# Splitting one 2 MB weight transfer at six of 32 experts into 8 + 8 + 112 partitions, in a hybrid decoder step on one Trainium2 core

## The chip, the core and the metric

The program runs on one core of one Trainium2 chip. Time is the device time of the program in microseconds (us). Before the change, three runs gave 1109.86, 1110.63 and 1121.22 us, with a median of 1110.63 us. Engines are named as in the profile: PE is TensorE, DVE VectorE, ACT ScalarE, POOL GpSimd, SP SyncE. SP issues nearly all transfers, and 16 DMA engines carry them.

## What is computed

One decoder layer for 256 prompt tokens and 8 x 4 sample tokens, all in float32: a normalisation and a combined projection, sliding-window attention beside a state-space part, an output projection, and then a mixture of experts. The last part takes most of the time:

```python
h = xb @ w_gate_up[e] + b_gate_up[e]          # 1024 -> 2048
return _clamped_swiglu(h) @ w_down[e] + b_down[e]   # 1024 -> 1024
...
y = jax.ops.segment_sum(out.astype(jnp.float32) * row_w[:, None], row_tok, num_segments=t_)
```

There are 32 experts, each token goes to four of them, and every expert's weights are read once: 8 MB for gate and up, 4 MB for down, 384 MB in all. The state-space part also returns its last states, `h_last`, an array of 128 partitions x 288 numbers (144 KB).

## The kernel before

The core works through the 32 experts one after the other, in 32 "positions". The position says how many tokens the expert is expected to have: `few` (a slim tile of 32 slots), `mid` (a wide tile of 64) or `many` (both). The kinds follow a fixed pattern: two `mid`, then four rounds of `few, many, few, mid`, then two rounds of `few, mid, mid, few, mid, mid`, then two `few`. Every engine runs the rounds as loops (`ROUNDS` = 4 and `LATER` = 2).

Weights go through two rings in SBUF. `gu_ring` has four slots of 2 MB; the four together hold one expert's gate and up weights. `dn_ring` has four slots of 2 MB: slots 0 and 1 take the down weights of even positions, slots 2 and 3 those of odd ones. A slot is 128 partitions x 16 KB, and one transfer fills it: partition p receives 16 KB that lie together in HBM (`load_gu` L341, `load_dn` L346). Before each transfer SP waits until PE has used the slot's old contents: it waits for `gu_used` in `gu` and for `dn_used` in `dn`. For each position SP issues the two down slots and then the four gate-up slots, in a loop at L394 that handles two positions each time and runs 14 times. Positions 0 and 1 are loaded ahead of the loop by `first_gu` (L352) and `first_dn` (L370), the last two behind it.

On PE a position is: `gate_up` (eight pieces of the inner dimension, k = 0 to 7, two for each gate-up slot, waiting for `gu_in` at each slot), turns and gathers, and `down` (four pieces, two for each down slot, waiting for `dn_in` at each slot). In `down` at a `few` position, `slim_part(c)` does piece c; c = 0 waits for the first down slot and c = 2 for the second.

Each transfer raises its semaphore by 16 when it has landed, and one semaphore belongs to one slot.

`h_last` is stored by POOL at its program's end (L2182), as soon as DVE has written it. SP passes a wait for the same event (`hlast_ready`) a little before L352's sixth transfer. Further on, SP waits for `out_done` to reach 64 (four earlier stores have landed) before it overwrites the memory those stores read.

Of the kernel before, what the change touches and what calls it, by code (L numbers as in the profile page):

```python
# [38 lines left out]
MT = 96  # L39
# [2 lines left out]
ITEMS = T * TOPK // SLOTS  # L42
PAIRS = NE // 2
GU_SLOTS = 4
GU_ROWS = KT // GU_SLOTS
FEW = 32
BODY, ROUNDS = ("few", "many", "few", "mid"), 4
# [30 lines left out]
def build(nc, a):  # L78
# [49 lines left out]
    o = REST  # L128
# [140 lines left out]
    for n in ("par_in cols_in b_in ones_in const_in c_in mask_in cache_in wglu_in wout_in "  # L269
              "w1_in late_in out_done "  # L270

              "xsq_ready xg_ready sum_ready ms_ready r_mix_ready u_proj un_ready u_ready proj_done proj_free "
              "sq_ready qk_sum vs_ready rq_ready qk_ready v_ready v_turned v_tok_ready "

              "par_dve par_act w1c_ready v_zero_ready v_power bt_turned bt_ready k_ready kd_ready tz_ready "
              "mag4_ready r_scan_ready x_ready x_free hin_ready hlast_ready "
              "y_done y_ready ysq_ready y_poly tanh_ready gelu_ready "

              "score_ready score_used neg_ready exp_done sum_inv p_ready pt_turned pt_ready pv_ready a_part_ready "
              "asq_ready asum_ready qs_ready av_ready ar_ready cleared outA_done xmid_ready "  # L280

              "glu_done ga_ready th_glu s_ready ssq_ready ssum_ready sv_ready sr_ready sn_ready outB_done x2_ready "

              "x2sq_ready rt_ready x2sum_ready x2v_ready r2sum_ready xn_ready logits_ready xtok_turned xtok_ready top_ready "
              "exp4_done sel_ready pos_ready "

              "bias_turned bias_ready order_ready "
              "first_half first_copied "
              "oh_ready gathered gath_ready xe_turned xe_ready gu_used g_acc g_copied l_copied h_turned "
              "h_step hg_ready th_ready h_ready dn_used ye_ready "  # L290
              "oh_s_ready gather_s copied_s raw_s_ready h_turned_s hg_s_ready th_s_ready h_s_ready ye_s_ready "
              "goh_s_ready g_turned_s gT_s_ready "
              "goh_ready g_turned gT_ready comb_done acc_done "
              "list_ready pos_item_ready h_out "
              "dve_order act_order").split():
        S(n)
    wu_in, wq_in = [S(f"wu_in{c}") for c in range(CT)], [S(f"wq_in{c}") for c in range(3)]
    S("tail_done"), S("dn_last")
# [73 lines left out]
    def load_others(sp):  # L372

        regs = [sp.alloc_register(f"sp_at{k}") for k in range(2)]

        def expert_at(k, p):
            sp.reg_load(regs[k], ord_e[0:1, p:p + 1] if isinstance(p, int) else ord_e[0:1, bass.ds(p, 1)])
            return sp.snap(regs[k], min_val=0, max_val=NE - 1)

        def gu(x, p_before):  # L380
            for k in range(GU_SLOTS):
                sp.wait_ge(S("gu_used"), p_before * 8 + GU_ROWS * (k + 1))
                load_gu(sp, x, k)

        def dn(x, p_before, j):
            for h in range(2):
                sp.wait_ge(S("dn_used"), p_before * 4 + 2 * (h + 1))
                load_dn(sp, x, h, j)

        for r in range(KT):  # L390
            sp.wait_ge(S("gu_used"), r + 1)
            first_gu(sp, 1, [r])
        sp.wait_ge(S("order_ready"), 1)
        with sp.Fori(0, PAIRS - 2) as i:  # L394
            x = [expert_at(k, i * 2 + (k + 2)) for k in range(2)]
            dn(x[0], i * 2, 0)
            gu(x[0], i * 2 + 1)
            dn(x[1], i * 2 + 1, 1)
            gu(x[1], i * 2 + 2)
        x = [expert_at(k, NE - 2 + k) for k in range(2)]  # L400
        dn(x[0], NE - 4, 0)
        gu(x[0], NE - 3)
        gu(x[1], NE - 2)
        for h in range(2):
            sp.wait_ge(S("dn_used"), (NE - 3) * 4 + 2 * (h + 1))
            if h == 0:
                load_dn(sp, x[1], 0, 1)
# [50 lines left out]
    def _(sp):  # L458
# [42 lines left out]
        first_gu(sp, 0, range(0, 5))  # L501
        sp.wait_ge(S("y_done"), 4)
        sp.wait_ge(S("hlast_ready"), 2)
        first_gu(sp, 0, range(5, 6))
        first_dn(sp, 0)
        sp.wait_ge(S("outA_done"), KT)
        sp.dma_start(w_out[:], a["w_out"][:, CT:2 * CT]).then_inc(S("wout_in"), 16)

        sp.wait_ge(S("glu_done"), 8)
        sp.wait_ge(S("out_done"), 64)  # L510
        first_gu(sp, 0, range(6, 8))
        first_dn(sp, 1)
        sp.wait_ge(S("sn_ready"), CT)
# [19 lines left out]
        for k, c in enumerate((0, 2, 1, 3)):  # L533
# [4 lines left out]
        sp.wait_ge(S("out_done"), 16 * 8)  # L538


    @block.tensor
    def _(pe):
# [447 lines left out]
        def down(w, s, kind, after, s_after, j, fill):  # L990

            def wide_part(c):
                if c == 0:
                    pe.wait_ge(S("h_ready"), w + 1)
                if c % 2 == 0:
                    pe.wait_ge(dn_in[2 * j + c // 2], fill * 16)
                for kk in range(2):
                    f = 2 * c + kk
                    for h in range(2):
# [5 lines left out]
            def slim_part(c):  # L1005
# [5 lines left out]
                    pe.wait_ge(S("dn_last"), 16)  # L1011
                if kind == "few" and c % 2 == 0:
                    pe.wait_ge(dn_in[2 * j + c // 2], fill * 16)
                for kk in range(2):
                    f = 2 * c + kk
                    for q in range(4):
# [75 lines left out]
        def expert(p, w, s, kind, before, after, j, fill):  # L1092
# [40 lines left out]
            down(w, s, kind, after, s_after, j, fill)  # L1133

        first_gather()
        turn_first()
# [2 lines left out]
        with pe.Fori(0, ROUNDS) as i:  # L1139
            for k in range(4):  # L1140
                expert(i * 4 + (2 + k), i * (WIDE[6] - WIDE[2]) + WIDE[2 + k], i * (SLIM[6] - SLIM[2]) + SLIM[2 + k],
                       BODY[k], BODY[k - 1], BODY[(k + 1) % 4], k % 2, i * 2 + (k // 2 + 2))
        with pe.Fori(0, LATER) as i:
            for k in range(6):
                p = FIRST_LATE + k
                expert(i * 6 + p, i * (WIDE[p + 6] - WIDE[p]) + WIDE[p], i * (SLIM[p + 6] - SLIM[p]) + SLIM[p],
                       KINDS[p], KINDS[p - 1], KINDS[p + 1], k % 2, i * 3 + (p // 2 + 1))
# [25 lines left out]
    def _(act):  # L1173
# [215 lines left out]
        for u in range(6):  # L1389
# [7 lines left out]
            if u == 3:  # L1397

                act.wait_ge(S("top_ready"), 1)
                A(ex4[0:MT], ex4[0:MT], ACT.Exp).then_inc(S("exp4_done"), 1)  # L1400

        def act_gathered(g):

# [130 lines left out]
    def _(dve):  # L1534
# [391 lines left out]
        dve.wait_ge(S("exp4_done"), 1)  # L1926
# [238 lines left out]
    def _(pool):  # L2165
# [140 lines left out]
```

## Time and profile before

| | |
|---|---|
| median of 3 runs | 1110.63 us |
| the profiled execution's own time | 1110.5 us |
| its span (first to last instruction) | 1108.7 us |
| granted TensorE clock, mean | 0.980 |
| PE busy | 986.8 us (89%) |
| DVE busy / ACT busy / POOL busy | 392.4 / 205.2 / 13.3 us |
| moved by DMA | 425.22 MB |

The page's slice row of DMA shows, for each fortieth of the span (27.7 us), how much of the time the 16 DMA engines were busy on average. A 9 is 90% or more. From the eighth slice on it reads 9 to the last but one. The share of a window is that of all 16 engines together: a 5 in it can mean that each engine works half the time, or that eight of them work and eight have nothing left.

### The profile page before, as it was taken

How to read it: one execution, taken by the hardware profiler on the slowest of the kernel's cores; microseconds unless marked ns; L12 is line 12 of the kernel's file. 1: busy time of each engine (PE TensorE's matmuls, PEld its weight loads, DVE VectorE, ACT ScalarE, POOL GpSimd, SP SyncE). 2: the span in 40 equal slices, each digit the busy share in tenths (PEclk: the TensorE clock that was granted, in tenths of full speed). 3: DMA queues.
4: the chain of work that ended last, by engine and by line, in shares of the span. 5: the costliest groups of instructions: out<-in, count | busy, mean ns of one | idle time of the engine just before them, and what ended most of it. 6: DMA issues, size and time to landing. Idle time of an engine off the chain costs nothing.

```text
span 1108.7 us, 16624 instructions
## 1 busy us (share of the span) xinstructions
PE 986.8 (89%) x6604; PEld 421.0 (38%) x6604; DVE 392.4 (35%) x898; ACT 205.2 (19%) x446; POOL 13.3 (1%) x11
## 2 busy tenths in 40 slices
PE   6999999999998999889997999799789879979976
PEld 5777764333332333233332233233233223323322
DVE  6987546231322132213222133123333323222222
ACT  4875333110111111111111011011111111101111
POOL 3000000000000000000000000000000000000000
PEclk9989999999999999999999999899999999999999
DMA  9424954999999999999999999999999999999996
GB/s 365 121 62 130 428 235 173 380 424 428 410 430 424 426 429 427 426 427 427 422 427 427 427 421 428 428 427 427 428 428 427 426 427 428 428 427 427 427 418 245
DMA packets 43132, 425.22 MB, mean 384 GB/s; under 512 B 11412, under 2 KB 14612, under 8 KB 16560
## 3 DMA queue, kind: packets, MB, share of 16 engines
q1 hardware_dynamic: 41280, 421.82, 91.0%
q10 hardware_dynamic: 1728, 2.11, 0.5%
q8 instruction: 63, 1.03, 0.4%
q0 software_dynamic: 48, 0.15, 0.0%
q14 instruction: 13, 0.11, 0.0%
HBM read 419.86 MB, written 2.51 MB: 381 GB/s over the span
## 4 chain that ended last, share of the span: by engine, by line
PE 56%; DMA 35%; DVE 4%; issue 2%; ACT 2%; ACTq 1%; DVEq 0%; SPq 0%
PE banks L544 53%; DMA gu_ring<-w_gu_dram 35%; PE banks L961 1%; DVE raw L1970 1%; PE banks L912 0%; DVE hl L1982 0%; DVE hT L1987 0%; PE banks L968 0%; PE banks L680 0%; PE banks L1038 0%; PE banks L1045 0%; ACT raw_s L1449 0%; ACT gath L1405 0%; ACT pT L1317 0%; DVE hl L1979 0%
## 5 line engine op out<-in xcount | busy, mean ns | idle before, releaser
L544 PE MATMUL banks<-gu_ring,xe 128*64 128x512 f32 x1152 | 271.4, 609 | 12.3 <-DMA gu_ring<-w_gu_dram 12.1
L2016 DVE TENSOR_TENSOR xT<-xT,banks 128x576 f32<-128x576 f32 x128 | 91.0, 751 | 534.1 <-PE banks L544 534.1
L544 PE MATMUL banks<-gu_ring,xe_s 128*32 128x512 f32 x1152 | 153.4, 626 | 48.1 <-DMA gu_ring<-w_gu_dram 35.8
L544 PEld LDWEIGHTS banks<-gu_ring,xe 128*64 128x64 f32 x1152 | 76.5, 138 | 168.7 <-issue 142.8
L544 PE MATMUL banks<-dn_ring,hT 128*64 128x512 f32 x576 | 129.3, 597 | 5.0 <-DVE hT L1987 5.0
L544 PEld LDWEIGHTS banks<-gu_ring,xe_s 128*32 128x32 f32 x1152 | 29.1, 111 | 138.4 <-issue 86.7
L544 PE MATMUL banks<-dn_ring,hT_s 128*32 128x256 f32 x1152 | 67.8, 381 | 3.3 <-ACT xe_s L1439 3.2
L544 PEld LDWEIGHTS banks<-dn_ring,hT 128*64 128x64 f32 x576 | 39.2, 137 | 79.4 <-issue 73.0
L1420 ACT ACTIVATE raw<-banks 128x512 f32<-128x512 f32 x18 | 10.7, 597 | 227.6 <-PE banks L544 227.6
L544 PE MATMUL banks<-x_tok,oh 96*64 96x512 f32 (+1 forms) x228 | 50.3, 578 | 0.4 <-DVE oh L1941 0.4
L544 PEld LDWEIGHTS banks<-dn_ring,hT_s 128*32 128x32 f32 x1152 | 35.0, 110 | 36.2 <-issue 15.1
L544 PE MATMUL banks<-gT,ye 64*128 64x288 f32 x288 | 46.8, 445 | 0.0
L1449 ACT ACTIVATE raw_s<-banks 128x512 f32<-128x512 f32 x18 | 10.7, 597 | 168.2 <-PE banks L544 168.2
L544 PE MATMUL banks<-xg,w_in 128*128 128x288 f32 x160 | 39.8, 406 | 0.0
L544 PEld LDWEIGHTS banks<-gT,ye 64*128 64x128 f32 x288 | 25.8, 193 | 34.6 <-issue 30.7
L1429 ACT ACTIVATE ye<-banks 128x512 f32<-128x512 f32 x18 | 10.7, 597 | 136.0 <-PE banks L544 136.0
L544 PE MATMUL banks<-aT,w_out 128*128 128x288 f32 x128 | 32.5, 409 | 2.8 <-DVE xT L1799 1.8
L544 PEld LDWEIGHTS banks<-xg,w_in 128*128 128x128 f32 x160 | 30.4, 190 | 8.4
L1970 DVE COPY raw<-banks 128x512 f32<-128x512 f32 x18 | 12.4, 692 | 53.6 <-PE banks L544 53.6
L961 PE MATMUL banks<-ident,raw 128*128 128x128 f32 x144 | 26.8, 309 | 2.2
L544 PE MATMUL banks<-gT_s,ye_s 32*128 32x288 f32 x288 | 27.3, 451 | 0.6 <-ACT ye_s L1458 0.6
L544 PEld LDWEIGHTS banks<-aT,w_out 128*128 128x128 f32 x128 | 23.9, 190 | 10.3 <-DVE xT L1799 2.2
(356 smaller groups left out, 857.4 us busy)
## 6 DMA issues: line engine op xcount, KB each, us to landing
gu_ring<-w_gu_dram SPq DMA_DIRECT2D x120, 2048.0 KB, 24.2
dn_ring<-w_dn_dram SPq DMA_DIRECT2D x63, 2048.0 KB, 21.5
gu_ring<-w_gu_dram SPq DMA_DIRECT2D x16, 1024.0 KB, 8.5
w_out<-w_out_dram SPq DMA_DIRECT2D x2, 2048.0 KB, 10.0
w_in<-w_in_dram SPq DMA_DIRECT2D x3, 1024.0 KB, 16.2
w_in<-w_in_dram SPq DMA_DIRECT2D x4, 512.0 KB, 9.9
w_glu<-w_glu_dram SPq DMA_DIRECT2D x1, 2048.0 KB, 8.9
dn_ring<-w_dn_dram SPq DMA_DIRECT2D x2, 1024.0 KB, 23.9
```

Source lines behind the costliest of these rows:

```text
L544: return nc.tensor.matmul(out, lhsT, rhs, start=start, stop=stop, **kw)
L961: last = pe.transpose(pb[2 + part][:, c * P:(c + 1) * P], hidden_cols(raw[:, part], c), ident[:])
L1420: A(blocks_out(raw[:, 0]), blocks_in(pb[0]), ACT.Copy).then_inc(S("g_copied"), 1)
L1429: A(ye[:], pb[4][:], ACT.Copy, scale=0.5).then_inc(S("ye_ready"), 1)
L1449: A(blocks_out(raw_s[:]), blocks_in(pb[5]), ACT.Copy).then_inc(S("raw_s_ready"), 1)
L1970: X.tensor_copy(blocks_out(raw[:, 1]), blocks_in(pb[1])).then_inc(S("l_copied"), 1)
L2016: X.tensor_tensor(two, two, pair[(1, 3)[n % 2]].rearrange("p (h f) -> p h f", h=2)[:, :, 0:T], ALU.add).then_inc(S("acc_done"), 1)
```

## The change

There are three edits.

1. At the first position of each round (positions 2, 6, 10, 14 of the four-position rounds, 18 and 24 of the six-position ones; all are `few`) the second down slot, `dn_ring[1]`, is filled by three transfers in place of one: partitions 0 to 7, partitions 8 to 15, and partitions 16 to 127. The first two raise a new semaphore, `dn_low`, and the third raises `dn_in[1]`. PE waits for both there. To have these positions apart, SP's loop becomes two loops, over rounds of four and of six positions.
2. `h_last` is stored by SP, ahead of the sixth `first_gu` transfer, and not by POOL. It now counts in `out_done`, whose later waits rise from 64 to 80 and, at the end, by 16.
3. Two semaphores (`exp4_done`, `h_out`) are gone. `exp4_done` is replaced by the eighth count of `exp_done`.

```diff
+        def dn_split(x, p_before):
+            sp.wait_ge(S("dn_used"), p_before * 4 + 2)
+            load_dn(sp, x, 0, 0)
+            sp.wait_ge(S("dn_used"), p_before * 4 + 4)
+            src = a["w_dn"][bass.ds(x, 1), 2:4].rearrange("o c p k f -> (o c p k) f").rearrange("(p i) f -> p i f", i=4)
+            for r in range(0, LOW, 8):
+                sp.dma_start(dn_ring[1][r:r + 8], src[r:r + 8]).then_inc(S("dn_low"), 16)
+            sp.dma_start(dn_ring[1][LOW:], src[LOW:]).then_inc(dn_in[1], 16)
...
-        with sp.Fori(0, PAIRS - 2) as i:
-            x = [expert_at(k, i * 2 + (k + 2)) for k in range(2)]
-            dn(x[0], i * 2, 0)
-            gu(x[0], i * 2 + 1)
-            dn(x[1], i * 2 + 1, 1)
-            gu(x[1], i * 2 + 2)
+        with sp.Fori(0, ROUNDS) as i:
+            for k in range(0, len(BODY), 2):
+                two_experts(i * len(BODY) + (2 + k), k == 0)
+        with sp.Fori(0, LATER) as i:
+            for k in range(0, len(LATE), 2):
+                two_experts(i * len(LATE) + (FIRST_LATE + k), k == 0)
...
         sp.wait_ge(S("hlast_ready"), 2)
+        sp.dma_start(a["h_last"][:], h_last[:]).then_inc(S("out_done"), 16)
         first_gu(sp, 0, range(5, 6))
...
-        sp.wait_ge(S("out_done"), 64)
+        sp.wait_ge(S("out_done"), 80)
...
                 if kind == "few" and c % 2 == 0:
                     pe.wait_ge(dn_in[2 * j + c // 2], fill * 16)
+                if kind == "few" and c == 2 and low is not None:
+                    pe.wait_ge(S("dn_low"), low)
...
-        pool.wait_ge(S("hlast_ready"), 2)
-        pool.dma_start(a["h_last"][:], h_last[:]).then_inc(S("h_out"), 16)
-        pool.wait_ge(S("h_out"), 16)
```

The order of SP's program at the head of its loop, before the change. `dn_ring_53` and `dn_ring_54` are the first and second down slot, `gu_ring_49` the first gate-up slot; an ISA row with "waits" is a wait by itself.

```order
L346 ISA [waits dn_used]
L346 DMA dn_ring_53<-w_dn_dram 128x4096
L387 REGISTER_ALU
L346 ISA [waits dn_used]
L346 DMA dn_ring_54<-w_dn_dram 128x4096
L382 ISA
L341 ISA [waits gu_used]
L341 DMA gu_ring_49<-w_gu_dram 128x4096
```

And the same place after it:

```order
L347 ISA [waits dn_used]
L347 DMA dn_ring_53<-w_dn_dram 128x4096
L398 REGISTER_ALU
L401 ISA [waits dn_used]
L401 DMA dn_ring_54<-w_dn_dram 8x4096
L401 ISA
L401 DMA dn_ring_54<-w_dn_dram 8x4096
L402 ISA
L402 DMA dn_ring_54<-w_dn_dram 112x4096
L383 ISA
L342 ISA [waits gu_used]
L342 DMA gu_ring_49<-w_gu_dram 128x4096
```

One transfer has become three behind the same wait, and no row of the gate-up slots has moved against them.

On PE, the down multiplications of the first position of a round, before:

```order
L544 MATMUL banks<-dn_ring_53,hT_s 32x256 [waits dn_in0]
L544 MATMUL banks<-dn_ring_53,hT_s 32x256 x15
L544 MATMUL banks<-dn_ring_54,hT_s 32x256 [waits dn_in1]
L544 MATMUL banks<-dn_ring_54,hT_s 32x256 x15
L937 ISA [waits copied_s,xe_ready]
L544 MATMUL banks<-gu_ring_49,xe 64x512 [waits gu_in0]
```

And after:

```order
L562 MATMUL banks<-dn_ring_53,hT_s 32x256 [waits dn_in0]
L562 MATMUL banks<-dn_ring_53,hT_s 32x256 x15
L1035 ISA [waits dn_in1]
L562 MATMUL banks<-dn_ring_54,hT_s 32x256 [waits dn_low]
L562 MATMUL banks<-dn_ring_54,hT_s 32x256 x15
L955 ISA [waits copied_s,xe_ready]
L562 MATMUL banks<-gu_ring_49,xe 64x512 [waits gu_in0]
```

The one wait ahead of the second slot has become two, and nothing else has moved on PE.

## Rows read from the trace of the kernel before

**Rows 1.** The page: the span, and busy share and rate of the 40 slices

```profile
span 1108.7 us, 16624 instructions
...
DMA  9424954999999999999999999999999999999996
GB/s 365 121 62 130 428 235 173 380 424 428 410 430 424 426 429 427 426 427 427 422 427 427 427 421 428 428 427 427 428 428 427 426 427 428 428 427 427 427 418 245
```

**Rows 2.** Who waited for whom on PE, 296 to 1075 us: total, times, longest

```profile
PE banks L544 <- DMA gu_ring<-w_gu_dram: 45.5, 29, 3.4
PE banks L544 <- issue: 12.3, 7, 2.4
...
PE banks L544 <- ACT xe_s L1439: 2.1, 3, 0.7
```

**Rows 3.** DMA, 296 to 1075 us: packets, MB, share of the time of 16 engines

```profile
DMA packets 22816, 332.33 MB, mean 427 GB/s; under 512 B 2530, under 2 KB 2530, under 8 KB 2530
...
q1 hardware_dynamic: 22764, 331.52, 100.2%
q8 instruction: 47, 0.77, 0.4%
q14 instruction: 5, 0.04, 0.0%
```

**Rows 4.** DMA, 1080 to 1100 us in 40 slices of 0.5 us

```profile
DMA  9989999999989999999977654545545455420000
GB/s 426 426 360 426 459 492 393 393 393 393 508 360 459 393 426 426 442 393 442 442 311 328 262 229 180 229 197 213 213 197 229 180 246 229 164 98 33 0 0 0
```

**Rows 5.** DMA, 288 to 300 us in 40 slices of 0.3 us

```profile
DMA  7989797979797979789352973595989898989999
```

**Rows 6.** SP's issues, 200 to 340 us: start, duration, line, operation

```profile
203.87 3.76 SPq L346 DMA_DIRECT2D dn_ring<-w_dn_dram  x2
...
293.71 4.06 SPq L346 DMA_DIRECT2D dn_ring<-w_dn_dram  x2
...
316.51 2.06 SPq L346 DMA_DIRECT2D dn_ring<-w_dn_dram  x2
```

**Rows 7.** SP's issues into dn_ring: ns min/median/max, first and last start; time to landing

```profile
L346 SPq MOVE dn_ring<-w_dn_dram x59: 29/29/38, 203.8 to 1073.2; - x59
L346 SPq DMA_DIRECT2D dn_ring<-w_dn_dram x59: 332/333/353, 203.9 to 1073.3; - x59
...
DMA to landing us min/median/max: 7.7/21.6/26.9
```

**Rows 8.** What SP waited for: total, times, longest

```profile
SPq L341 <- PE banks L544: 473.6, 120, 13.1
SPq L346 <- PE banks L544: 288.2, 58, 11.5
```

**Rows 9.** DMA, 37 to 47 us: small transfers into 16 partitions each

```profile
DMA packets 2249, 0.51 MB, mean 51 GB/s; under 512 B 2249, under 2 KB 2249, under 8 KB 2249
...
q1 hardware_dynamic: 2249, 0.51, 31.9%
```

**Rows 10.** The store of h_last on POOL, and its time to landing

```profile
L2182 POOL DMA_DIRECT2D h_last_dram<-h_last x1: 688/688/688, 100.9 to 100.9; - x1
...
DMA to landing us min/median/max: 2.2/2.2/2.2
```

**Rows 11.** DMA, 120 to 150 us in 40 slices of 0.75 us

```profile
DMA  9999999999999999999998996100000000987999
```

**Rows 12.** PE at the last gate-up landing: start, duration, and the wait before it

```profile
1089.39 1.06 PE L544 MATMUL banks<-gu_ring,xe_s 128*32 128x512 f32 x8 [2.36 <-DMA gu_ring<-w_gu_dram]
```

More of the change, by code:

```diff
@@ L44 @@
 GU_SLOTS = 4
+LOW = 16
 GU_ROWS = KT // GU_SLOTS
@@ L284, in build @@
               "x2sq_ready rt_ready x2sum_ready x2v_ready r2sum_ready xn_ready logits_ready xtok_turned xtok_ready top_ready "
-              "exp4_done sel_ready pos_ready "
+              "sel_ready pos_ready "
               "bias_turned bias_ready order_ready "
@@ L293, in build @@
               "goh_ready g_turned gT_ready comb_done acc_done "
-              "list_ready pos_item_ready h_out "
+              "list_ready pos_item_ready "
               "dve_order act_order").split():
@@ L297, in build @@
     wu_in, wq_in = [S(f"wu_in{c}") for c in range(CT)], [S(f"wq_in{c}") for c in range(3)]
-    S("tail_done"), S("dn_last")
+    S("tail_done"), S("dn_last"), S("dn_low")
     gu_in = [S(f"gu_in{k}") for k in range(GU_SLOTS)]
@@ L393, in load_others, with two_experts @@
         sp.wait_ge(S("order_ready"), 1)
-        with sp.Fori(0, PAIRS - 2) as i:
-            x = [expert_at(k, i * 2 + (k + 2)) for k in range(2)]
-            dn(x[0], i * 2, 0)
-            gu(x[0], i * 2 + 1)
-            dn(x[1], i * 2 + 1, 1)
-            gu(x[1], i * 2 + 2)
+        def dn_split(x, p_before):
[6 more added lines that the diff above has]
+            sp.dma_start(dn_ring[1][LOW:], src[LOW:]).then_inc(dn_in[1], 16)
+        def two_experts(p, split):
+            x = [expert_at(k, p + k) for k in range(2)]
+            (dn_split if split else dn)(x[0], p - 2, *(() if split else (0,)))
+            gu(x[0], p - 1)
+            dn(x[1], p - 1, 1)
+            gu(x[1], p)
+        with sp.Fori(0, ROUNDS) as i:
[4 more added lines that the diff above has]
+                two_experts(i * len(LATE) + (FIRST_LATE + k), k == 0)
         x = [expert_at(k, NE - 2 + k) for k in range(2)]
@@ L537, in _ @@
             sp.dma_start(a["y"][:, c::4], xT[:, c::4]).then_inc(S("out_done"), 16)
-        sp.wait_ge(S("out_done"), 16 * 8)
+        sp.wait_ge(S("out_done"), 16 * 9)
     @block.tensor
@@ L988, in combine_last, with down @@
                 last.then_inc(S("comb_done"), 1)
-        def down(w, s, kind, after, s_after, j, fill):
+        def down(w, s, kind, after, s_after, j, fill, low=None):
             def wide_part(c):
@@ L996, in wide_part @@
                     pe.wait_ge(dn_in[2 * j + c // 2], fill * 16)
+                if c == 2 and low is not None:
+                    pe.wait_ge(S("dn_low"), low)
                 for kk in range(2):
@@ L1013, in slim_part @@
                     pe.wait_ge(dn_in[2 * j + c // 2], fill * 16)
+                if kind == "few" and c == 2 and low is not None:
+                    pe.wait_ge(S("dn_low"), low)
                 for kk in range(2):
@@ L1090, in gate_bias, with expert @@
                     last.then_inc(S("comb_done"), 1)
-        def expert(p, w, s, kind, before, after, j, fill):
+        def expert(p, w, s, kind, before, after, j, fill, low=None):
             w_before, s_before = w - (before != "few"), s - (before != "mid")
@@ L1132, in expert @@
                 residual(LAST_PARTS[2])
-            down(w, s, kind, after, s_after, j, fill)
+            down(w, s, kind, after, s_after, j, fill, low)
         first_gather()
@@ L1141, in _ @@
                 expert(i * 4 + (2 + k), i * (WIDE[6] - WIDE[2]) + WIDE[2 + k], i * (SLIM[6] - SLIM[2]) + SLIM[2 + k],
-                       BODY[k], BODY[k - 1], BODY[(k + 1) % 4], k % 2, i * 2 + (k // 2 + 2))
+                       BODY[k], BODY[k - 1], BODY[(k + 1) % 4], k % 2, i * 2 + (k // 2 + 2),
+                       (i * (2 * LOW) + 2 * LOW) if k == 0 else None)
         with pe.Fori(0, LATER) as i:
@@ L1146, in _ @@
                 expert(i * 6 + p, i * (WIDE[p + 6] - WIDE[p]) + WIDE[p], i * (SLIM[p + 6] - SLIM[p]) + SLIM[p],
-                       KINDS[p], KINDS[p - 1], KINDS[p + 1], k % 2, i * 3 + (p // 2 + 1))
+                       KINDS[p], KINDS[p - 1], KINDS[p + 1], k % 2, i * 3 + (p // 2 + 1),
+                       (i * (2 * LOW) + 2 * LOW * (ROUNDS + 1)) if k == 0 else None)
         expert(NE - 2, N_WIDE, N_SLIM - 2, "few", "mid", "few", 0, PAIRS)
@@ L1399, in _ @@
                 act.wait_ge(S("top_ready"), 1)
-                A(ex4[0:MT], ex4[0:MT], ACT.Exp).then_inc(S("exp4_done"), 1)
+                A(ex4[0:MT], ex4[0:MT], ACT.Exp).then_inc(S("exp_done"), 1)
         def act_gathered(g):
@@ L1924, in _ @@
         X.tensor_reduce(sel[M], by_token, AX.X, ALU.add).then_inc(S("sel_ready"), 1)
-        dve.wait_ge(S("exp4_done"), 1)
+        dve.wait_ge(S("exp_done"), 8)
         link(X.tensor_reduce(gs[M], ex4[M], AX.X, ALU.add))
```

## The prediction

> **What bounds the kernel now.** I read the page's slices first. From the eighth slice to the last but one DMA is at 9 tenths and moves about 427 GB/s, flat, while the experts run [rows 1]. Then the waits on PE in that stretch: of all that PE waits for between 296 and 1075 us, the largest is the landing of a gate-up slot, 45.5 us in 29 waits; no row names a down slot [rows 2]. Then the transfers of the stretch: SP's queue filled 100.2% of the time of the 16 DMA engines [rows 3]. So the engines' work sets the pace, and a transfer is complete only when the last of them has done its part.
>
> What the mean hides is in the tail. The last weights are issued by 1075 us. At 1080 to 1090 us all 16 engines are busy. Behind 1090 us the share falls to 5 tenths and stays there until about 1097.5 us, at half the rate, about 200 GB/s [rows 4]. I read it as eight engines that have finished and eight that have 7 to 8 us left, though each got the same number of rows: every weight transfer is 128 partitions. An alternative reading, that all 16 run at half rate at the end, is unlikely, since they ran at full rate with the same transfers until 1090 us. Something else has held one half back. The only other traffic in the stretch is 47 + 5 instruction transfers, with 0.4% of the time [rows 3]. If these go mostly to one half, the tail of 7.5 us x 8 engines = 60 engine-us over 52 transfers makes 1.15 us for each, a plausible price for 16 KB that breaks into a stream.
>
> In the Trainium skill, "Runtime: NRT & Kernel Launch", section "Instruction fetch mechanics", each sequencer fetches its instructions by its own DMA queue in blocks of 16 KiB; the rows agree (0.77 MB in 47 transfers), but neither says on which DMA engines.
>
> **The price of a row.** 331.52 MB in rows of 16,384 bytes are 20,234 rows; 16 engines x 779 us / 20,234 = 0.616 us for a row on one engine [rows 3]. A plain slot costs every engine 8 rows, 4.93 us.
>
> **The split.** 112 partitions divide by 16: seven rows for each engine. Eight partitions do not, so a transfer of them can occupy at most eight engines with a row each. If both small ones take the same eight engines, these do 9 rows in that slot and the others 7. Each split gives the one half one row more and the other one less. The late half then finishes 0.616 us earlier for each split, provided that it never runs dry. Not all six count. At 293 to 296 us the share falls to 3 and 2 tenths [rows 5]: for a moment all engines wait for PE. Position 2's down slots are issued at about 204 us, those of position 6 not before 316.5 us [rows 6]. What position 2 gains is waited away at 294 us. Five splits are left: 5 x 0.616 = 3.1 us. The early half, 7.5 us ahead, gets 3.1 us more and is 7.5 - 6.2 = 1.3 us ahead at the end, so it does not become the bound.
>
> PE's landings from position 6 on come earlier by up to 3.1 us, and PE has room to follow: it waits 45.5 us for them [rows 2]. Its work behind the last landing does not change, so the whole end moves.
>
> **Which eight.** The Trainium skill, "DMA: Bandwidth & Descriptors", section "Why a DMA increments its semaphore by 16 and not by 1", says that such a transfer runs on the largest number of engines up to 16 that divides the row count, and on the lowest-numbered ones; by that both small transfers fall on the same eight, as assumed above. No row carries an engine's number, so whether these are the early or the late half is open. I take the early half, as a guess, at better than two to one; the other case is a rival.
>
> **Issues on SP.** Two more transfers at each split: 2 x (0.333 + 0.029) = 0.72 us [rows 7]. SP waits 762 us for PE over the kernel [rows 8] and a down slot lands 21.6 us after its issue, so the queue in front of the engines hides it: 0. Without that cover it would be 6 x 0.72 = 4.3 us. Behind the split's issues the first gate-up slot is issued up to 0.72 us later, and its landing follows the queue, not the issue. SP's longer loops may cost some more instruction transfers; at 1.15 us on one of eight engines each would put 0.14 us on the late half. I allow ten at most, 1.4 us, and take 0.
>
> **The second wait on PE.** One more wait instruction at six positions. SP's register move takes 0.029 us [rows 7]; PE's next stop is a gate-up landing that it waits for anyway. 0, at most 0.2 us. The small transfers are issued ahead of the 112, so `dn_low` is no later than `dn_in[1]`, and neither is waited for, by the absence of dn_ring in rows 2.
>
> **The store of h_last.** It leaves POOL, where its 0.69 us and 2.2 us to landing end at about 104 us [rows 10], long before the program's end: nothing is gained. On SP it stands ahead of one gate-up and two down transfers; 144 KB at 427 GB/s are 0.35 us, and one issue is 0.33 us. DMA has nothing to do from about 140 to 145 us [rows 11], which swallows it: 0. If it were not, 0.7 us. The renamed semaphores cost nothing: the same events are counted.
>
> **Sum.** 0 + 0 + 0 - 3.1 us, against the profiled execution's own 1110.5 us: 1107.4 us. That execution lies 0.1 us below the median of the runs.
>
> **Rival 1: few partitions take their rows slowly.** Eight engines write into eight neighbouring partitions at once. The nearest rows are transfers into 16 partitions: 2249 packets take 31.9% of 16 x 10 us, 51.0 us, for 0.51 MB, so 0.100 us for a KB [rows 9]; the weight rows take 0.616 / 16.4 = 0.0376. Part of that factor of 2.7 is the small packets' own overhead. Lower bound 1 (a row still 0.616 us), upper bound 2.7 (1.64 us). For the low half each split then costs 0.616 + 2 x 1.02 = 2.67 us, five of them 13.3 us, less its lead of 7.5: it ends 5.8 us behind the old end, at 1116.3 us. The gain is gone when a small row takes 0.616 + 0.44 = 1.06 us (3.1 + 10 x 0.44 = 7.5), and that decides the sign. I take the lower bound, since I hold rows 9 to be mostly overhead of packets under 512 bytes, but with doubt.
>
> **Rival 2: four neighbouring partitions share one way in.** The weight rows show what one engine moves into one partition at a time, not whether four engines can write into four neighbouring ones at that rate each. If the four together get the rate of one, a small row takes 4 x 0.616 = 2.46 us, 1.85 us more [rows 3], and the low half ends 3.1 + 10 x 1.85 - 7.5 = 14.1 us behind the old end: 1124.6 us. For it: in rows 9 a KB is dear with only 16 partitions written. Against it: rows 9 are small packets, and eight engines that don't start in step collide for less than the whole row. The Trainium skill, "SBUF — State Buffer", section "Door 1: The DMA port swizzle", has this rule: partitions 0 to 3 lie on one of 16 ports and 4 to 7 on another. No run here shows it so far.
>
> **Rival 3: the low eight are the late half.** Then it gets 3.1 us more: 1113.6 us.
>
> **Rival 4: no shift.** The small transfers are spread over changing engines, or the rows of the 112-partition part, which no longer go to the same engines as in a plain slot, disturb each other: five splits x 7 rows are 35 rows on an engine, and 0.09 us more on each eats the 3.1 us. 1109 to 1111.5 us.
>
> **How the numbers follow.** Forecast (1106.4 to 1108.4 us by itself) 0.48; rival 1 (1109 to 1116.3 us) 0.11; rival 2 (above 1120 us) 0.10; rival 3 0.14; rival 4 0.14; anything else 0.03, of which 0.01 on the fast side. A measurement of this kernel can tell about 1%, 11 us, from no change. Only rival 2 leaves that band upward: slower 0.10. A gain of 11 us has no source in the rows: faster 0.01. The other 0.89 is no change that can be told. The range goes from 1105.4 us (forecast and 2 us for a late half that is uneven in itself) to 1116.4 us, rival 1's bound: it leaves out rival 2 and little else.
>
> **What would show it.** Right: in the tail DMA's share falls from 9 to near 0 within about 2 us, and PE starts on the last gate-up landing near 1086.3 us, now 1089.39 us [rows 12]. Rivals 1 and 2: a half-empty tail stays, PE's waits for gu_ring grow, and GB/s dips around each split. Rival 3: the half-empty tail is about 14 us long. Rival 4: the tail is as before. I am wrong altogether if PE shows waits for dn_ring, or if the stage ahead of the experts takes another time.

## The result, and the profile after

| | before | after |
|---|---|---|
| median of the runs, same chip, us | 1114.46 (1109.86 to 1121.22, 4 runs) | 1164.51 (1161.74 to 1165.09, 4 runs) |
| profiled execution's span, us | 1108.7 | 1163.1 |
| mean granted TensorE clock | 0.980 | 0.957 |
| PE's waits for gu_ring in the whole kernel, us | 47.8 in 30 | 100.7 in 49 |

The ratio is 1.0433 (95% interval 1.0393 to 1.0474): the change makes the kernel 50 us slower. I had forecast 1107.4 us and a range up to 1116.4. The kernel before comes out now near 1110, now near 1119 us, from run to run, and so do some of the variants below; their intervals hold this, and one run of a variant, 1552.06 us at a granted clock of 0.60, is left out of its median.

The page of the kernel after, the span and the DMA slices (29 us each). They answer to [rows 1].

```profile
span 1163.1 us, 16650 instructions
...
DMA  9415757999999999999999999999999999999985
GB/s 350 129 51 197 329 222 289 320 425 428 426 325 426 427 427 372 350 428 417 428 343 428 427 385 335 418 427 428 427 427 392 336 424 425 425 418 428 419 326 219
```

Where before the rate stood flat at 427 GB/s, it now dips in slices 12, 16 and 17, 21, 24 and 25, and 31 and 32. These are five of the six positions with a split; the first, at 207 us, falls into the eighth slice (320 GB/s, before 380). DMA's busy share stays at 9 tenths in all of them. The engines are not short of work: they move less while they are busy.

The waits on PE and the DMA totals of the kernel after, from 296 us to the issue of the last weights, 1130 us. They answer to [rows 2] and [rows 3].

```profile
PE banks L562 <- DMA gu_ring<-w_gu_dram: 100.2, 48, 9.9
```

```profile
DMA packets 23126, 335.63 MB, mean 402 GB/s; under 512 B 2638, under 2 KB 2638, under 8 KB 2638
...
q1 hardware_dynamic: 23072, 334.80, 99.3%
q8 instruction: 47, 0.77, 0.4%
q14 instruction: 7, 0.06, 0.0%
```

The mean rate is 402 GB/s at 99.3% busy. Against 427 GB/s this is (427 - 402) / 427 x 834 us = 49 us, and PE's waits for gate-up slots have grown by 52 us. That is most of the 54.4 us between the spans of the two profiled executions. The first split, ahead of this stretch, costs as well: between 200 and 240 us the queue moves 13.37 MB, before it was 15.61, which is 5.2 us; between 240 and 300 us it wins 1.0 us back (25.56 MB against 25.15). 49 + 4 makes 53 us. The instruction transfers are as many as before (47 in q8).

The lower clock is not the cause. PE's busy time has grown by 13.4 us (986.8 to 1000.2 us) as the mean granted clock fell from 0.980 to 0.957, but PE waits 100 us for gate-up slots at the same time, and in the dip shown next the granted clock is 1.00.

Now one split close up. SP issues it at 318.7 us. The transfers of the kernel after between 318 and 358 us, in 40 slices of 1 us:

```profile
DMA  9999999999999999989999999899989999999999
GB/s 442 442 393 426 426 426 426 442 442 393 426 442 442 393 459 328 262 172 229 213 246 213 213 213 262 197 229 229 246 229 377 426 393 459 426 393 459 410 410 442
...
q1 hardware_dynamic: 984, 14.03, 100.0%
```

And the queue's total of the kernel before in the same stretch, where the rate is flat:

```profile
q1 hardware_dynamic: 1162, 16.94, 99.8%
```

From 334 to 348 us the rate is about half, 197 to 262 GB/s with one slice of 172, while DMA's share stays at 8 or 9 tenths. In these 40 us 16.94 - 14.03 = 2.9 MB less are moved, 6.8 us of work at 427 GB/s. The dip lasts 15 us, three times what a slot takes.

The trace also keeps a record of every packet, with start, duration and size. None carries an engine's number, but in the full stream each starts 3 or 4 ns before another has ended, and that links them into 16 sequences, as many as there are engines; a packet of 4 bytes closes each transfer in a sequence. Read in this way, the records of this split show three things:

- Eight sequences have one row of each small transfer and seven of the large one, the other eight have seven rows alone: 9 and 7, as the prediction had it.
- The rows of 16 KB between 334 and 346 us took 1.09 to 1.50 us, with a median of 1.17, where they took 0.61 us in the kernel before. That holds in all 16 sequences, and for the rows of the plain slots ahead of the split's and behind them too.
- The first sequence enters the split's rows at about 333 us and the last leaves them at 347.8 us. That is the dip. At the last split the first enters at about 896 us and the last leaves at 913.7 us, 18 us, since the engines are further apart there.

The page's list of DMA issues of the kernel after: KB each, us to landing.

```profile
dn_ring<-w_dn_dram SPq DMA_DIRECT2D x57, 2048.0 KB, 23.1
...
dn_ring<-w_dn_dram SPq DMA_DIRECT2D x6, 1792.0 KB, 31.2
```

The 112-partition parts land after 31.2 us, the plain slots after 23.1.

SP's issues into dn_ring in the kernel after: ns min/median/max, first and last start. They answer to [rows 7].

```profile
L347 SPq DMA_DIRECT2D dn_ring<-w_dn_dram x53: 332/333/356, 203.6 to 1129.7; - x53
...
L401 SPq DMA_DIRECT2D dn_ring<-w_dn_dram x12: 286/310/343, 207.0 to 890.8; - x12
...
L402 SPq DMA_DIRECT2D dn_ring<-w_dn_dram x6: 322/322/323, 208.0 to 891.3; - x6
```

An issue of eight partitions takes 0.31 us, one of 112 takes 0.32. No PE wait names dn_ring.

The last 45 us of the kernel after, in 40 slices of 1.1 us. They answer to [rows 4].

```profile
DMA  9999998209799999998999810001000000799200
GB/s 364 437 393 437 466 422 350 102 29 291 320 393 422 437 452 422 437 422 364 415 437 430 350 58 29 29 29 36 7 0 0 0 15 0 269 329 386 72 0 7
```

The tail is no longer half empty for 7.5 us. From 1147 to 1150 us it moves 29 GB/s, which is one engine's rate (427 / 16 = 27): a single engine is behind. Between 1128 and 1130 us the share falls to 2 and 0: SP's next issues go out only at 1129 to 1130 us, and until then the engines have nothing to do.

### The profile page after: what moved, and what is told of

It is laid out like the page before. It is cut to its first block, busy times and chain, and to the rows that moved or that the text cites. A ratio compares the mean times of both kernels' runs of the same rounds, so it can differ in the third digit from the quotient of the medians.

```text
span 1163.1 us, 16650 instructions
## 1 busy us (share of the span) xinstructions
PE 1000.2 (86%) x6604; PEld 423.8 (36%) x6604; DVE 392.2 (34%) x898; ACT 205.2 (18%) x446; POOL 12.6 (1%) x10
## 4 chain that ended last, share of the span: by engine, by line
PE 48%; DMA 45%; DVE 4%; ACT 1%; issue 1%; ACTq 1%; SPq 0%; DVEq 0%
PE banks L562 45%; DMA gu_ring<-w_gu_dram 45%; PE banks L979 1%; DVE raw L1994 0%; PE banks L698 0%; PE banks L930 0%; PE banks L986 0%; DVE hl L2006 0%; DVE hT L2011 0%; PE banks L1067 0%; PE banks L1060 0%; ACT raw_s L1473 0%; ACT pT L1341 0%; ACTq L1207 0%; ACT gath L1429 0%
## 5 line engine op out<-in xcount | busy, mean ns | idle before, releaser
L562 PE MATMUL banks<-gu_ring,xe 128*64 128x512 f32 x1152 | 271.9, 610 | 23.1 <-DMA gu_ring<-w_gu_dram 23.0
L562 PE MATMUL banks<-gu_ring,xe_s 128*32 128x512 f32 x1152 | 162.4, 671 | 77.7 <-DMA gu_ring<-w_gu_dram 77.7
L562 PE MATMUL banks<-gT,ye 64*128 64x288 f32 x288 | 49.4, 465 | 0.0
## 6 DMA issues: line engine op xcount, KB each, us to landing
dn_ring<-w_dn_dram SPq DMA_DIRECT2D x57, 2048.0 KB, 23.1
dn_ring<-w_dn_dram SPq DMA_DIRECT2D x6, 1792.0 KB, 31.2
```

The source lines that it names most:

```text
L562: return nc.tensor.matmul(out, lhsT, rhs, start=start, stop=stop, **kw)
```

## The experiments

They ran in three groups, each beside its own runs of the kernel before; a ratio is always to those. The diffs are against the kernel after, and show SP's part; where the number of transfers on `dn_low` changes, the count that PE waits for changes with it. The first group asks which part of the change costs: the code around the split, the number of transfers, or their shape.

**No split.** All the edits stay, but each slot is one transfer.

```
-            (dn_split if split else dn)(x[0], p - 2, *(() if split else (0,)))
+            dn(x[0], p - 2, 0)
...
-                if c == 2 and low is not None:
-                    pe.wait_ge(S("dn_low"), low)
```

> The changed kernel with every edit but the split: the second down slot of the six positions is again one transfer of 128 partitions, and PE's second wait is gone; SP's two longer loops and SyncE's store of h_last stay. Theory A (the shape of the split transfers costs the time): as before the change, 1110 to 1113 us. Theory C (the loops on SP, the extra waits or the store of h_last cost it): near the changed kernel's 1164 us, or a measurable part of it.

Measured: 1117.73 us (10 runs) against 1117.34 (19 runs), ratio 0.9988 (0.9959 to 1.0017). SP's longer loops, the renamed semaphores and the store of h_last by SP cost nothing. The whole 4.3% is in the split.

**Two transfers by columns.** The slot is cut in two, but both halves have all 128 partitions (8 KB of each).

```
-            for r in range(0, LOW, 8):
-                sp.dma_start(dn_ring[1][r:r + 8], src[r:r + 8]).then_inc(S("dn_low"), 16)
-            sp.dma_start(dn_ring[1][LOW:], src[LOW:]).then_inc(dn_in[1], 16)
+            sp.dma_start(dn_ring[1][:, 0:2], src[:, 0:2]).then_inc(S("dn_low"), 16)
+            sp.dma_start(dn_ring[1][:, 2:4], src[:, 2:4]).then_inc(dn_in[1], 16)
```

> The split along the other axis: two transfers of all 128 partitions with 8 KB each, six times, with the same second semaphore and wait. Theories A1, A2 and B: no loss, 1110 to 1113 us. Theory C (one more transfer and one more wait cost the time): near 1164 us.

Measured: 1118.05 us (8 runs), ratio 1.0003 (0.9966 to 1.0040). The kernel with two transfers by columns, 318 to 358 us:

```profile
GB/s 442 475 377 442 459 377 459 426 410 459 393 426 475 360 410 418 418 426 418 467 451 393 442 459 410 442 410 410 442 393 426 442 410 410 475 410 410 442 377 459
...
q1 hardware_dynamic: 1304, 16.97, 100.2%
```

There is no dip (16.97 MB, before 16.94). One more transfer, one more semaphore and PE's second wait cost nothing that can be told. What costs is the cut along the partitions.

**16 and 112 partitions.** The two small transfers become one.

```
-            for r in range(0, LOW, 8):
-                sp.dma_start(dn_ring[1][r:r + 8], src[r:r + 8]).then_inc(S("dn_low"), 16)
-            sp.dma_start(dn_ring[1][LOW:], src[LOW:]).then_inc(dn_in[1], 16)
+            sp.dma_start(dn_ring[1][0:16], src[0:16]).then_inc(S("dn_low"), 16)
+            sp.dma_start(dn_ring[1][16:], src[16:]).then_inc(dn_in[1], 16)
```

> The split as one transfer of partitions 0 to 15 and one of 16 to 127, six times. Theory A1 (the two transfers of eight partitions on eight engines are slow): nothing left of the loss, 1111 us. Theory A2 (in any transfer that is not all 128 partitions the engines no longer write each into partitions of its own, and get in each other's way): most of the loss stays, 1140 to 1160 us. Theory C: 1150 us or more.

Measured: 1161.22 us (2 runs), ratio 1.0390 (1.0324 to 1.0456), a little above theory A2's 1140 to 1160 us. The same stretch in this kernel:

```profile
GB/s 459 360 475 426 377 475 393 426 442 360 508 442 360 492 410 393 475 328 262 246 246 156 115 246 246 213 197 147 262 246 213 246 410 426 426 426 410 459 393 410
...
q1 hardware_dynamic: 966, 13.93, 99.7%
```

**64 and 64 partitions.** Both halves are large, and 64 rows divide evenly by 16.

```
-            for r in range(0, LOW, 8):
-                sp.dma_start(dn_ring[1][r:r + 8], src[r:r + 8]).then_inc(S("dn_low"), 16)
-            sp.dma_start(dn_ring[1][LOW:], src[LOW:]).then_inc(dn_in[1], 16)
+            sp.dma_start(dn_ring[1][0:64], src[0:64]).then_inc(S("dn_low"), 16)
+            sp.dma_start(dn_ring[1][64:], src[64:]).then_inc(dn_in[1], 16)
```

> The split as two transfers of 64 partitions, six times; both divide by 16, so every engine has four rows of each. Theory A1: 1111 us. Theory A2, with half of the partitions reached at half the rate: 8 rows of 0.616 us become 8 of 1.23 us, 4.9 us for each split, 1140 us. Theory B (an uneven number of rows on the engines costs it): 1111 us.

Measured: 1162.09 us (2 runs), ratio 1.0398 (1.0336 to 1.0459), the highest expectation passed by some 20 us. The same stretch in this kernel:

```profile
DMA  9999999999999999999899899799999899999999
GB/s 459 426 426 426 393 459 410 410 475 426 393 442 410 459 410 410 475 410 279 164 213 254 180 213 262 164 229 246 197 213 213 295 360 426 426 442 393 459 442 377
...
q1 hardware_dynamic: 983, 14.09, 99.9%
```

The two kernels lose what the kernel after loses (13.93 and 14.09 MB, after 14.03; before 16.94), and with 64 + 64 the share again stays at 8 or 9 tenths but for one slice. With 16 + 112 and with 64 + 64 no engine has more rows than another: by the packet records each of the 16 sequences has one and seven, or four and four. So it isn't the uneven number of rows, nor the smallness of a part.

The second group measures the parts one by one and leaves bytes out for that.

**The small transfers alone.** The 112 partitions are left out.

```
-            for r in range(0, LOW, 8):
-                sp.dma_start(dn_ring[1][r:r + 8], src[r:r + 8]).then_inc(S("dn_low"), 16)
-            sp.dma_start(dn_ring[1][LOW:], src[LOW:]).then_inc(dn_in[1], 16)
+            sp.dma_start(dn_ring[1][0:8], src[0:8]).then_inc(S("dn_low"), 16)
+            sp.dma_start(dn_ring[1][8:16], src[8:16]).then_inc(dn_in[1], 16)
```

> The two transfers of eight partitions alone; the one of 112 is left out, so at six positions 7/8 of the second down slot is not loaded. Without any contention the low eight engines have 6 rows less and the others 8 at each of these positions, so the kernel is no slower than before: 1095 to 1105 us. Theory A1 (eight neighbouring partitions share few ways in): a small row takes up to 2.46 us, and for 3 to 5 us at each split the rate is low, 1103 to 1111 us. Theory G (such a transfer slows all 16 engines): the rate of all falls to about half from its first row to its last, and the plain rows in flight take about 1.2 us.

**The small transfers alone, four partitions apart.** The same source rows in the same two transfers of eight, but their places in SBUF lie four partitions apart.

```
...
+            sp.dma_start(dn_ring[1][0:32:4], src[0:8]).then_inc(S("dn_low"), 16)
+            sp.dma_start(dn_ring[1][1:33:4], src[8:16]).then_inc(dn_in[1], 16)
```

> As e5_small_only, from the same eight rows of HBM each, but written to partitions 0, 4, ..., 28 and 1, 5, ..., 29 and not to neighbours (so the weights lie in wrong places, too). If the cost lies where the rows are written (A1), a small row takes 0.61 us and the dip at the split is gone; if it lies in the source, in the number of rows or in the use of eight engines, the dip is that of e5_small_only.

Measured: neighbours 1110.49 us (8 runs), four apart 1096.26 us (1093.87 and 1098.64), against 1116.55; ratios 0.9947 (0.9910 to 0.9983) and 0.9825 (0.9696 to 0.9953). Both leave out 112 of the slot's 128 rows, seven for an engine on average. Priced as in the prediction, with five positions that count, that is 5 x 7 x 0.616 = 21.6 us. Four apart gets 20.3 us of it, neighbours 6.1 us. The stretch of 318 to 358 us, first the neighbours, then four apart:

```profile
DMA  9998998998989989989997799999999999999999
GB/s 410 410 492 344 475 459 360 492 442 360 492 377 410 492 377 442 459 344 508 344 147 147 131 246 344 328 344 418 442 410 442 410 426 442 393 426 442 410 426 459
...
q1 hardware_dynamic: 1088, 15.66, 100.1%
```

```profile
DMA  9999999999999999999999998999999999999989
GB/s 410 426 410 459 442 410 426 459 426 410 410 426 442 426 426 442 393 442 475 393 426 442 426 451 360 459 426 393 459 459 393 442 393 442 442 377 442 442 360 492
...
q1 hardware_dynamic: 1179, 17.02, 100.1%
```

Two transfers of 128 KB into neighbours pull the rate to 147 and 131 GB/s for three slices, at a share of 9 tenths. The same bytes written four partitions apart leave no mark, and 1.4 MB more are moved. By the packet records even an engine with no small row is held up by the neighbours: its eight plain rows behind the small transfers took 7.8 us instead of 4.9. Source, size and number are the same in both, so where the rows are written decides. The price of being neighbours is 1110.49 - 1096.26 = 14.2 us by the medians (two runs of one of them) and 17.7 us by the two profiled executions, so about 3 us for each split.

**The 112 partitions alone.** The small ones are left out.

```
-            for r in range(0, LOW, 8):
-                sp.dma_start(dn_ring[1][r:r + 8], src[r:r + 8]).then_inc(S("dn_low"), 16)
...
-                if c == 2 and low is not None:
-                    pe.wait_ge(S("dn_low"), low)
```

> The transfer of partitions 16 to 127 alone; the two small ones are left out, so 1/8 of the second down slot is not loaded at six positions. Without contention every engine has one row less: 1107 us. Theory A2 (a transfer that is not all partitions puts engines in each other's way): most of the 45 to 50 us stay, 1140 to 1155 us, and the dip lasts 9 to 12 us. Theory A1 alone: 1107 us.

Measured: 1159.06 us (1153.14 and 1164.98), ratio 1.0388 (1.0211 to 1.0565), though an eighth of the slot isn't loaded; theory A2 had said 1140 to 1155 us. The same stretch in this kernel:

```profile
GB/s 442 393 475 393 426 426 393 442 459 377 475 426 393 492 328 229 246 246 197 229 180 221 213 262 197 164 246 426 442 393 426 442 360 492 426 393 459 393 393 492
...
q1 hardware_dynamic: 992, 14.43, 100.0%
```

The rate is half for 12 us, without any small transfer. The 112-partition part alone makes most of the loss: 1159.06 - 1116.55 = 42.5 us of 50, with two runs that lie 12 us apart. The prices don't add up (42.5 + 14 is more than 50), so the two share part of one slowdown.

**A quarter of the slot in 64 + 64.** Three quarters of each partition come by one transfer of 128.

```
-            for r in range(0, LOW, 8):
-                sp.dma_start(dn_ring[1][r:r + 8], src[r:r + 8]).then_inc(S("dn_low"), 16)
-            sp.dma_start(dn_ring[1][LOW:], src[LOW:]).then_inc(dn_in[1], 16)
+            sp.dma_start(dn_ring[1][:, 0:3], src[:, 0:3]).then_inc(dn_in[1], 16)
+            for r in range(0, P, 64):
+                sp.dma_start(dn_ring[1][r:r + 64, 3], src[r:r + 64, 3]).then_inc(S("dn_low"), 16)
```

> Three quarters of the slot's columns as one transfer of 128 partitions with 12 KB each, the last quarter as two of 64 partitions with 4 KB each, six times. If the cost goes with the bytes that take the uneven way: a quarter of e3_64_64's 45 us, 11 us, so 1125 to 1130 us. If every departure from the plain shape costs a fixed time: 1160 us.

Measured: 1131.75 us (1127.53 and 1135.97), ratio 1.0143 (0.9992 to 1.0294). The interval just holds no change; that there is a loss is shown by the trace. The same stretch in this kernel:

```profile
GB/s 492 393 377 492 377 442 410 426 475 393 410 459 397 393 418 340 238 209 205 315 262 442 426 442 410 442 410 426 442 393 459 377 442 442 393 426 459 393 459 410
...
q1 hardware_dynamic: 1257, 15.93, 100.1%
```

The dip is 5 to 6 us long, and 16.94 - 15.93 = 1.0 MB is lost in it, 2.4 us; with the whole slot in 64 + 64 it was 2.85 MB. A quarter of the bytes costs about a third. The price goes with the bytes that travel in the uneven shape, and isn't a fixed sum for each transfer.

The third group asks whether the shift of rows between engines, on which the forecast rested, can be had without the dip. Only positions 18 and 24 are split. Of their slot, three quarters go by one transfer of 128 partitions, the last quarter by 16 transfers of eight. If a transfer of eight runs on eight engines, the low eight then do the work of 10 rows and the others that of 6.

**Sixteen transfers of eight, four apart.** All bytes go to their right places.

```
+            sp.dma_start(dn_ring[1][:, 0:3], src[:, 0:3]).then_inc(dn_in[1], 16)
+            for q in range(0, P, 32):
+                for r in range(4):
+                    sp.dma_start(dn_ring[1][q + r:q + r + 29:4, 3], src[q + r:q + r + 29:4, 3]).then_inc(S("dn_low"), 16)
...
-                two_experts(i * len(BODY) + (2 + k), k == 0)
+                two_experts(i * len(BODY) + (2 + k), False)
```

> A split without neighbours, at positions 18 and 24 only: three quarters of the slot's columns as one transfer of 128 partitions, the last quarter (4 KB rows) as 16 transfers of eight partitions that lie four apart. The low eight engines then do the work of 10 rows in that slot, the others of 6. If the low eight are the early half and nothing else costs: 2 x 2 x 0.616 = 2.5 us less, 1108 us, and the half-empty tail of 7.5 us shrinks to 2.6 us. If they are the late half: 1113 us and a tail of 12 us. If engines that write into another half's partitions disturb it there: up to 1.2 us more for each split. The loss of the changed kernel, 7 us and more for each split, does not come back.

**The same with eight neighbours.**

```
+            sp.dma_start(dn_ring[1][:, 0:3], src[:, 0:3]).then_inc(dn_in[1], 16)
+            for r in range(0, P, 8):
+                sp.dma_start(dn_ring[1][r:r + 8, 3], src[r:r + 8, 3]).then_inc(S("dn_low"), 16)
```

> As e9_apart_low, the same bytes, engines and number of transfers at positions 18 and 24, but each small transfer takes eight neighbouring partitions. If writing into neighbours is what costs: a 4 KB row takes 4 x 0.154 us, 7.4 us more for the low eight at each split, 1118 to 1127 us, and the rate dips at the two splits. If it isn't: the time of e9_apart_low.

Measured: four apart 1125.88 us (1124.31 to 1126.65, 3 runs), ratio 1.0114 (1.0057 to 1.0171); neighbours 1127.13 us (2 runs), ratio 1.0121 (1.0064 to 1.0178); the kernel before 1112.86. Both expectations of the first are missed, and where the rows are written makes hardly a difference in this form: rows of 4 KB in 16 transfers that follow each other. So the finding from the small transfers holds for the two transfers of 16 KB rows that it was measured on, and isn't a law for all.

The stretch of the second split, 860 to 940 us, in slices of 2 us, first in the kernel with four apart, then the queue's total of the kernel before:

```profile
GB/s 410 442 418 442 418 432 360 369 225 360 414 365 260 426 393 442 442 393 442 426 434 410 442 426 426 418 451 434 410 410 438 426 418 451 418 401 426 451 426 410
...
q1 hardware_dynamic: 2503, 32.72, 99.9%
```

```profile
q1 hardware_dynamic: 2338, 34.05, 100.2%
```

1.33 MB are lost at this split, 3.1 us. The first split loses 2.6 us: SP issues it from 679 us, and between 680 and 740 us 24.45 MB are moved, before it was 25.58. With neighbours the first split loses 1.51 MB and the second 1.20, 6.3 us in all against 5.7.

The end of the kernel with four apart, then of that with neighbours, 1080 to 1125 us in slices of 1.1 us:

```profile
DMA  9999999999998999999996642111000003798000
GB/s 408 422 451 437 437 437 393 393 437 466 393 459 379 437 422 451 393 430 408 393 422 291 255 204 95 51 51 58 22 0 0 0 15 128 251 381 289 0 7 0
```

```profile
DMA  9989999999999998999999997311110000006993
GB/s 393 451 379 437 408 451 379 437 408 408 393 408 451 422 459 379 422 437 422 408 430 401 430 401 313 153 73 58 51 51 29 0 0 0 0 15 225 327 387 110
```

Before the last engines stop, the rate is 51 to 58 GB/s for 5 us: two engines' rate. In the kernel before, it was 200 GB/s, eight engines' [rows 4]. So six of the eight that were late no longer are, and two still are: the eight that got more rows must be for the most part early ones, and not all. The packet records of the kernel with neighbours agree: at the plain slot just ahead of the second split, seven of the eight sequences that carry the 4 KB rows end at 867.5 to 868.9 us and one at 870.5 us, and the other eight end at 868.9 to 871.0 us. A shift that loads a late engine can't bring the end forward.

Where do the 13.0 us come from? Some 7 us of them are not the split's. In the profiled execution with four apart, SP's first issue in its loop is at 211.0 us, in that of the kernel before at 203.9 us, and both are ahead of any split. From 60 to 80 us the granted clock there is 0.55 and 0.50 (near the lower of its two levels, 1.2 GHz), and in the kernel before 1.00 and then 0.56. The profiled kernel with no split has the same late start, at 211.6 us, and a span of 1116.7 us. Against that one the 1122.4 us with four apart are 5.7 us more, which is what the two dips lose; nothing is left for the two late engines. This early stretch also looks like the source of the runs near 1119 us, though only the profiled executions show it.

## Why the prediction was wrong

**The stage that decides, and its price: right.** DMA's work set the pace before and does so after. 49 us are lost there by the rate and 4 at the first split, of 54.4 us between the two profiled executions, and PE's waits for gate-up grew by 52.

**SP's issues, PE's second wait, h_last, the semaphores: right, each 0.** No split at all came out at 0.9988, and twice the transfers by columns at 1.0003. PE never waits for dn_ring.

**The tail, and nine rows against seven: right.** Behind 1092.5 us eight rows are in flight at a time in the kernel before, so eight engines had finished, and the split dealt its rows 9 and 7. An instruction transfer of 16 KB was put at 1.15 us; in the packet records the 47 took a median of 1.07 us. That they fall mostly on the late half is not shown.

**The row at 0.616 us: the step that failed.** The prediction took it for every row, the 112 partitions' too, and let rival 4 put 0.09 us on these at most by the way it was priced. The dip shows otherwise. For 15 us everything moves at half the rate, and a row takes a median of 1.17 us on all 16 engines. It isn't only the split's 2 MB: 15 us at some 220 GB/s are 3.3 MB, and the plain slots next to it are slowed as well. Five dips of 6.8 to 8.6 us are 34 to 43 us, and the last slice of the stretch to 1130 us, at 316 GB/s and a share of 7 tenths, loses 21 x 111 / 427 = 5.4 us more, part of it while the engines have nothing to do; that nearly makes the 49. The 112-partition part alone gives 42.5 us. The prediction also let only five splits count, since a gain of the first is waited away at 294 us; of the first one's loss of 5.2 us some 4 stayed. Rival 4 named the right place ("the rows of the 112-partition part ... disturb each other"), but its size was set by what would eat the gain and not by a bound: the rows of before had no transfer of fewer than 128 partitions in a full stream, and the factor of 2.7 from [rows 9] that I put on the small rows should have been put on all the rows of the split. A factor of 2 on the slot's eight rows alone is 5 x 8 x 0.616 = 24.6 us, and had the range reached only as far, it would have said slower by 2%.

**Rivals 1 and 2: the mechanism fits, the place was too narrow.** Rival 1 slowed the small rows by up to 2.7 and reached 1116.3 us. Rival 2 said that neighbouring partitions share a way in, and charged only ten small rows on one half of the engines: 18.5 us and 3.1 us for the five more rows, less the half's lead of 7.5 us. That these 14.1 us come near the 14.2 us between neighbours and four apart is luck: there, engines without a small row are held up too. And the 112 partitions alone cost three times as much; rival 2 gave 1124.6 us where 1164.5 came. It stood at a chance of 0.10, so the range stopped at rival 1.

**Which ways are shared: what the runs show and what not.** The Trainium skill, "SBUF — State Buffer", section "Door 1: The DMA port swizzle", gives partitions 0 to 63 eight of the 16 ports and 64 to 127 the other eight, four neighbours one port, and says that a transfer of 128 partitions gives each port an engine of its own. The trace agrees where it can: 128 partitions in two transfers have no dip, rows four apart (eight ports) none, eight neighbours (two ports) do, and 64 + 64 do. By the count of ports alone 64 + 64 would be at half rate for its own 2 MB, an estimate from the page of 4.9 us lost for each split; measured were 2.85 MB, 6.7 us. And the 112 partitions reach all 16 ports, yet lose as much. That the plain rows of all 16 engines are held up while any engine is in such a part, is shown by the packet records. That it is so because the engines no longer have a port each, is argued here and not shown, and the 4 KB rows, which lose nearly as much four apart as side by side, don't fit it.

**The shift of rows: wrong.** "The low eight are the early half" was a guess at 2 to 1 between two pure cases, and neither holds: the engines that get more rows are mixed, most early and two late. With two late engines among them nothing was gained (5.7 us slower against an execution with an equal start). The signs named for the forecast are all absent: the tail ends on one lone engine, and not in 2 us on all of them. Of the signs for rivals 1 and 2 two came, the longer waits and the dips, and the half-empty tail did not.

**What stays open.** Why all 16 engines slow down together, the ones that are still on plain rows too, and why the two last kernels lose 5.7 and 6.3 us. Why the loss grows in the course of the kernel is answered in part: by the queue's totals it is 6.8 us at 318 us; behind the last split, at 891 us, the kernel after moves 30.39 MB between 860 and 940 us, where before it was 34.05, and that is 8.6 us. The dip lasts from the first engine's entry to the last one's exit, 15 and 18 us, so engines that drift apart make it longer; but no run holds them together to try it. Which engines carry the instruction transfers is open too.

None of the versions that compute the whole is faster than the kernel before.

## What to carry to other kernels

In a kernel whose DMA engines are full, cut a load along the free dimension and keep all 128 partitions in each part; a cut along partitions slowed the whole stream to half for three times the slot's own time. Look at GB/s and the busy share together: a full share at a falling rate is a stream that hinders itself, and no busy share shows it. When the trace has no row of the new shape, its widest factor belongs on every row of that shape, not only on the small ones.

## What the runs showed of the hardware

- Transfers that don't cover 128 partitions, in a full stream on one queue: half the rate for 12 to 20 us at a share of 7 to 9 tenths (8 + 8 + 112, 112 alone and 64 + 64 alike), 7 to 10 us lost for each slot of 2 MB; with 16 + 112 the last split lost 11.8 us in 25 (29.03 MB between 860 and 940 us, before 34.05). The rows of 16 KB, on all 16 engines, took a median of 1.17 us and not 0.61 (334 to 346 us in the kernel after), and the slow stretch lasts from the first engine's entry into the slot to the last one's exit. Two transfers of 128 partitions and half the columns: none.
- Two transfers of 128 KB (eight partitions each) cost about 3 us for each split when the partitions are neighbours, and nothing that can be measured four partitions apart; with 4 KB rows, 16 transfers in a row, it made hardly a difference (5.7 us apart, 6.3 us side by side, for two slots).
- An instruction transfer of 16 KB took a median of 1.07 us in the full stream of the kernel before (47 packets).
- An issue's length on SP: 0.31 us for eight neighbours, 0.33 for 128 partitions. In the kernels with 16 transfers of eight the issues took 0.277 us each with neighbours, and 0.645 us each with four apart:

```profile
L403 SPq DMA_DIRECT2D dn_ring<-w_dn_dram x32: 644/645/838, 679.0 to 872.4; - x32
```
